# Loading the last two modulation pieces by halves, splitting the first query/key unit by column halves, and one unit load moved ahead of six small loads

## What is computed

```python
ada = jax.nn.silu(c) @ w_ada[l] + b_ada[l]               # 6 x 1024 columns per layer
sh1, sc1, g1, sh2, sc2, g2 = jnp.split(ada, 6, axis=-1)
h = x * (1.0 + sc1) + sh1                                # 256 tokens x 1024
qa, ka, va, qb, kb, vb = jnp.split(h @ w_in, AB_SPLITS)  # queries, keys, values
# attention, output projection, layer norm, feed forward; a second layer; the second block
```

## Time and profile before

| | |
|---|---|
| median of 3 runs | 1247.75 us (1244.14 to 1251.18) |
| the profiled execution | 1245.37 us, its span 1243.7 us |
| TensorE busy | 1200.2 us, 96% of the span |
| VectorE busy | 675.1 us, 54% |
| ScalarE busy | 503.0 us, 40% |
| DMA | 394.98 MB, mean 318 GB/s |
| chain that ended last | PE 84%, DVE 8%, ACT 3%, DMA 3% |

### The profile page before, as it was taken

How to read it: one execution, slowest core, us unless ns; L and a number is a source line. 1 busy time by engine, 2 the same in 40 slices (tenths; PEclk the granted TensorE clock), 3 DMA queues, 4 the chain that set the end, 5 groups by cost and what they waited for, 6 DMA issues and landing times.

```text
span 1243.7 us, 16572 instructions
## 1 busy us (share of the span) xinstructions
PE 1200.2 (96%) x6586; PEld 827.0 (66%) x6586; DVE 675.1 (54%) x1222; ACT 503.0 (40%) x763; POOL 53.8 (4%) x103
## 2 busy tenths in 40 slices
PE   6999899999999999999999999999999999999997
PEld 2697688887789877888878787445544444454446
DVE  5689968887679786764566675211211111111126
ACT  1478654444555575344347384111111111111125
POOL 0100101000000000001001200000000000000000
PEclk9999999999999999999999999999999999999998
DMA  9997868988646455765557779999999999999990
GB/s 368 388 338 275 311 222 307 346 311 324 246 171 249 173 219 184 280 219 204 198 201 269 250 304 397 410 426 426 424 425 425 427 411 425 427 424 426 425 412 35
DMA packets 50987, 394.98 MB, mean 318 GB/s; under 512 B 6673, under 2 KB 8913, under 8 KB 11378
## 3 DMA queue, kind: packets, MB, share of 16 engines
q1 hardware_dynamic: 39618, 337.18, 67.7%
q0 software_dynamic: 9072, 53.92, 12.1%
q10 hardware_dynamic: 2240, 3.10, 1.0%
HBM read 390.68 MB, written 3.49 MB: 317 GB/s over the span
## 4 chain that ended last, share of the span: by engine, by line
PE 84%; DVE 8%; ACT 3%; DMA 3%; issue 1%; SPq 1%; ACTq 0%; DVEq 0%
PE psum L1357 18%; PE psum L770 10%; PE psum L773 10%; PE psum L777 10%; PE psum L1403 9%; PE psum L1289 5%; PE psum L1297 2%; PE psum L825 2%; PE psum L829 2%; PE psum L827 2%; DMA staged<-in_ada 2%; DVE w_parts L2113 2%; DVE aring L2096 1%; PE psum L1056 1%; PE psum L1068 1%; PE psum L1047 1%
## 5 line engine op out<-in xcount | busy, mean ns | idle before, releaser
L2113 DVE TENSOR_TENSOR w_parts<-w_raw,w_parts 128x2048 fp32r<-128x2048 f32 x106 | 241.7, 2287 | 73.1 <-ACT w_parts L1493 73.1
L1493 ACT ACTIVATE w_parts<-w_raw 128x2048 fp32r<-128x2048 f32 x106 | 202.0, 1911 | 80.5 <-DMA w_raw<-in_units 80.5
L1357 PE MATMUL psum<-slabs,arena 128*64 128x512 f32 x768 | 222.5, 592 | 0.0
L770 PE MATMUL psum<-w_parts,h_parts 128*128 128x512 f32 x416 | 165.7, 398 | 2.4 <-ACT h_parts L1493 1.3
L773 PE MATMUL psum<-w_parts,h_parts 128*128 128x512 f32 x416 | 163.2, 392 | 0.0
L1357 PEld LDWEIGHTS psum<-slabs,arena 128*64 128x64 f32 x768 | 71.8, 137 | 109.2 <-issue 109.1
L1493 ACT ACTIVATE arena<-psum 128x512 f32<-128x512 f32 (+1 forms) x43 | 23.8, 557 | 245.4 <-PE psum L1376 140.0
L777 PE MATMUL psum<-w_parts,h_parts 128*128 128x512 f32 x416 | 111.8, 391 | 0.7 <-DVE h_parts L2290 0.7
L2096 DVE CUSTOM_DVE_ANT_0 aring<-aring,cb 128x1024 f32<-128x1024 f32 x80 | 94.5, 1219 | 2.0 <-DMA aring<-in_ada 1.9
L770 PEld LDWEIGHTS psum<-w_parts,h_parts 128*128 128x128 f32 x416 | 78.6, 189 | 20.3 <-DVE w_parts L2113 2.1
L777 PEld LDWEIGHTS psum<-w_parts,h_parts 128*128 128x128 f32 x416 | 78.1, 188 | 17.8 <-DVE h_parts L2290 1.3
(11 more groups left out here) (333 smaller groups left out, 1878.0 us busy)
## 6 DMA issues: line engine op xcount, KB each, us to landing
w_raw<-in_units SPq DMA_DIRECT2D x110, 1024.0 KB, 5.2
slabs<-in_w SPq DMA_DIRECT2D x52, 1024.0 KB, 14.4
slabs<-in_w SPq DMA_DIRECT2D x22, 2048.0 KB, 20.0
aring<-in_ada POOLq DMA_DIRECT2D x40, 1024.0 KB, 5.6
arena<-in_w SPq DMA_DIRECT2D x16, 2048.0 KB, 18.8
w_odd<-in_w SPq DMA_DIRECT2D x16, 2048.0 KB, 19.2
w_odd<-in_w SPq DMA_DIRECT2D x24, 1024.0 KB, 24.1
staged<-in_ada SPq DMA_DIRECT2D x8, 1024.0 KB, 18.6
```

The costliest lines, as they stand in the source:

```text
L770: mm(psum[:, bank, :], high(tile, tok), w_hi(k)[:, col:col + 512], start=first and bank not in begun, stop=False, skip_group_check=True)
L1357: ins = nc.tensor.matmul(psum[s * CAP:(s + 1) * CAP, w, :], xe_t[:, kt, s * CAP:(s + 1) * CAP], up_weights(w, s, b, kt), start=kt == 0, st ...
L1493: return nc.scalar.activation(out_ap, in_ap, func, **kw)
L2113: v.tensor_tensor(w_lo(k), raw(k), w_hi(k).bitcast(F32), ALU.subtract).then_inc(w_split, 1)
```

## The change

Four edits in the opening, with what they need elsewhere.

1. The loads of pieces 6 and 7 are each cut into two transfers of 512 KB (`stage_half(n, t)`, the columns of `t` = 0 and of `t` = 1). The order on SP becomes: half 0 of piece 6, half 0 of piece 7, half 1 of piece 6, unit 3, half 1 of piece 7, unit 4. DVE handles them by halves (`last_scale(0)`, `last_scale(1)`) and gives `scale_ready` 4 for feature tile 6 and 5 for feature tile 7; ACT waits for each tile by itself.
2. `first_values` runs over the two feature tiles outside and the two token tiles inside, so that it needs the second feature tile only for its second half. The event `v_half` comes after three quarters of the last call, where it came after one half.
3. The split of unit 4 is done in two halves by column (128 x 1024 each) on ACT and on DVE; the first half of `to_heads(0, 0, 0)` waits for the first half alone.
4. Unit 5 (with its wait for `unit_done` 1) is issued ahead of the six small loads.

```diff
-            for i in range(4):
+            def stage_half(n, t):
+                col = slice(t * D, (t + 1) * D)
+                sp.dma_start(staged[n][:, col], a["ada"][ADA_ORDER[n]][:, col]).then_inc(last_half_in[n - 6] if t else staged_in[n], 16)
+
+            for i in range(3):
                 stage(2 * i)
...
+            stage_half(6, 0)
+            stage_half(7, 0)
+            stage_half(6, 1)
+            load_unit(3)
+            stage_half(7, 1)
             load_unit(4)
+            load_unit(5)
             small_loads(((lam_in[:], a["lam_in"]), (bias[:, 16, :], a["causal"]), (w_forget[:], a["w_forget"]),
...
-            for k in range(SLOTS, Z_AT):
+            for k in range(SLOTS + 1, Z_AT):
...
-                for t in range(TT):
-                    for s in range(2):
-                        pe.wait_ge(h_first, 2 * i + s + 1)
+                for s in range(2):
+                    pe.wait_ge(h_first, 2 * i + s + 1)
+                    for t in range(TT):
...
+                if k == QK_AT and s:
+                    weights(k)
                 if s == 0:
-                    weights(k)
+                    if k == QK_AT:
+                        pe.wait_ge(first_high, first_high_at)
+                        pe.wait_ge(first_low_half, first_low_at)
+                    else:
+                        weights(k)
...
-                act.wait_ge(scale_ready, p + 1)
                 for kt in (2 * p, 2 * p + 1):
-
+                    act.wait_ge(scale_ready, p + 1 if kt < KT - 1 else p + 2)
...
-            split(4)
+            act.wait_ge(w_loaded[slot_of(4)], 16)
+            for half_s in range(2):
+                ins = A(by_half(w_hi(4), half_s), by_half(raw(4), half_s), Cp)
+                if half_s == 0:
+                    ins.then_inc(first_high, 1)
+            ins.then_inc(w_hi_ready, 1)
...
+            def last_scale(t):
+                for n in (6, 7):
+                    dve.wait_ge(last_half_in[n - 6] if t else staged_in[n], 16)
+                    w = staged[n][:, t * D:(t + 1) * D]
+                    at_ = 2 * (n % 2) + t
+                    v.tensor_tensor_reduce(out=w, in0=w, in1=cb[:], scale=1.0, scalar=0.0, op0=ALU.mult, op1=ALU.add,
+                                           accum_out=ada_raw[:, at_:at_ + 1]).then_inc(ada_sum, 1)
+                dve.wait_ge(ada_sum, 12 + 2 * t + 2)
+                for n in (6, 7):
+                    at_, col = 2 * (n % 2) + t, 2 * ADA_ORDER[n] + t
+                    ins = v.tensor_tensor(ada_cols[:, col:col + 1], ada_raw[:, at_:at_ + 1], V("b_ada", col, 1), ALU.add)
+                    if t:
+                        ins.then_inc(ada_done, 1)
+                    else:
+                        link(ins)
+                if t:
+                    dve.wait_ge(ada_done, 8)
+                v.tensor_scalar(small[:, 6 + t:7 + t], ada[:, 0, 14 + t:15 + t], 1.0, None, ALU.add).then_inc(scale_ready, 1)
+
             first_scale(0)
             for p in range(3):
-                first_scale(p + 1)
+                if p < 2:
+                    first_scale(p + 1)
+                else:
+                    last_scale(0)
                 first_low(p)
...
+            last_scale(1)
             first_low(3)
-            split(4)
+            dve.wait_ge(first_high, first_high_at)
+            v.tensor_tensor(by_half(w_lo(4), 0), by_half(raw(4), 0), by_half(w_hi(4), 0).bitcast(F32),
+                            ALU.subtract).then_inc(first_low_half, 1)
+            dve.wait_ge(w_hi_ready, split_no(4))
+            v.tensor_tensor(by_half(w_lo(4), 1), by_half(raw(4), 1), by_half(w_hi(4), 1).bitcast(F32),
+                            ALU.subtract).then_inc(w_split, 1)
             split(5)
```

More of the change, by code:

```diff
@@ L337, in raw, with by_half @@
             return w_raw[:, slot_of(k), 0, :]
+        def by_half(unit, s):
+            return unit.rearrange("p (k s n) -> p s k n", s=2, n=P)[:, s, :, :]
         def w_lo(k):
@@ L361, in build @@
         scale_ready, h_first = sem("scale_ready"), sem("h_first")
+        first_high, first_high_at = h_first, KT + 1
+        first_low_half, first_low_at = scale_ready, 6
         h_high, h_low = sem("h_high"), sem("h_low")
@@ L424, in build @@
         sg_done, out_ready, stored = sem("sg_done"), [sem("out_ready0"), sem("out_ready1")], sem("stored")
+        last_half_in = (ple_in, late_rows)
         COPIES, BANDS = 32, 16 * P // 32
@@ L806, in first_values @@
                                      skip_group_check=True)
-                    if i == 3 and t == 0:
-                        ins.then_inc(v_half, 1)
+                        if i == 3 and s == 1 and t == 0:
+                            ins.then_inc(v_half, 1)
                 ins.then_inc(unit_done, 1)
@@ L1227, in _ @@
                 from_act(layer, 10, 1)
-            pe.wait_ge(ple_in, 16)
+            pe.wait_ge(ple_in, 32)
             pe.wait_ge(early_rows, 32)
@@ L2927, in _ @@
             root("gate", 1)
-            dve.wait_ge(late_rows, 32)
+            dve.wait_ge(late_rows, 48)
             gated_sum(0, 0, cols[0])
```

## The result

The change made the kernel slower: 1249.65 us, median of 21 runs (1247.06 to 1252.54), against 1244.69 us for the kernel before (1243.37 to 1251.18, 21 runs beside them). The ratio over all runs of both is 1.0035, 95% interval 1.0027 to 1.0043, so 3.4 to 5.4 us are lost where I had forecast a gain of 1.2. The profiled execution has a span of 1246.4 us.

What follows compares the result with a forecast made beforehand. TensorE, busy for 96% of the span, was taken as the bound; of at most 1.87 us direct gain, a lead of 1.5 fell to 1.2: 1245.37 - 1.2 = 1244.2 us profiled, 1246.5 for the median; range 1242.3 to 1250.5.

Steps and rivals of the forecast that it cites:

- my rivals: Whole kernel: lead lost again, 1247.5 us, chance 0.24; more gained, 1245.5, 0.13; transfers cost more, 1250.8, 0.08.
- The halves of pieces 6 and 7: Opening loads: first halves by 34.49, last half 40.3, fourth value call at 39.2 instead of 41.05; lead 1.5 us.
- the slower rival: Opening loads: two more transfers cost 3.6 us, last half lands at 43.9; 2.0 to 3.6 lost, 1250.8 us; chance 0.08.
- Bytes and queue are the same, only the order differs.: Loads of pieces 6 and 7: half a piece takes 1.50 us, against 3.00 for a piece.
- that page's sum per transfer: Skill page: a DMA costs about 2.0 us plus bytes over 436 GB/s; would put unit 4 at 47.0; forecast took zero.
- Then unit 4 at 42.99 as before: Opening loads: after the last half at 40.3, unit 4 lands at 42.99, unchanged.
- that cover: ACT's unit 4 split and first value copy end at 46.0 against PE's need at 46.4; any overrun paid one for one.
- Unit 6 follows the same bytes as before and lands at 53.72: Loads after unit 5 and the small loads: unit 6 split by 57.95 against a need at 58.0, just met.
- The sum: Whole kernel: 1245.37 - 1.2 = 1244.2 us for the profiled execution, 1246.5 for the median; forecast's chance 0.55.
- Column halves, order of the matmuls, extra instructions: Unit 4 split halves 1.0 us on ACT, 1.2 on DVE; same 16 matmuls; extra DVE work (3 x 0.17) mostly in waits.
- I let the 1.2 us stand to the end.: After the first scores: the 1.2 us PE lead becomes a DVE lead near 92 us and lasts to the end.
- What I named as proof against me: Opening: last half after 41, unit 3 holding PE at 39.2, unit 5 near 49, no PE lead at layer norm, 153.

## Why the prediction was wrong

The measured time lies inside the range that I gave, but on the other side of no change, and the mechanism that decided it was none of my rivals. That the range holds it is luck: it reached so far for a fixed cost of each transfer, which did not occur, and for the spread of a median.

- **The halves of pieces 6 and 7.** Right within 0.3 us: both first halves by 34.72 and the last half at 40.41, for 34.5 and 40.3; the fourth call at 39.00 for 39.2, held by unit 3 by 0.19; a call longer by 0.4 (7.49 against 7.10) for a pause of 0.35 in its middle. The last half came before 41.9, so the slower rival, a fixed cost for each transfer, did not occur.
- **"Bytes and queue are the same, only the order differs."** This is the first step that failed. The packets are not the same. On SP's queue 7.1 KB went in a packet with whole pieces, 3.6 KB with halves, and in the same stretch ACT's copy sent a packet for each. I counted bytes on SP's queue and never looked at what ACT's and POOL's queues were waiting for. The Trainium skill has the rule, in DMA: Bandwidth & Descriptors, section Queues, rings and completion order: each DMA engine goes round the queues that have work and takes a packet from each in turn. By that rule the traces agree to one packet in 200. I weighed that page's sum per transfer and passed over this. In that page of the Trainium skill the sum stands in section Anatomy of one DMA, not in Measured as I wrote, and it is for transfers issued from GpSimd, which these were not. The last half at 40.41, for 40.3 from bytes alone, shows no such cost.
- **"Then unit 4 at 42.99 as before".** It was 45.11, by the early bands, whose turns and lower total rate I had no term for; with the bands at 41.32 it was in by 43.54. The lead ended there: ACT's split and its value copy behind it came 1.26 us late for PE. I had put that cover at 0.4 us and named the price, one for one; it was paid. Unit 5 followed 4.6 us after unit 4 where I had 4.3, so its 49.70 for 47.3 is unit 4's delay.
- **"Unit 6 follows the same bytes as before and lands at 53.72"**, and the sentence that the small loads are late "by one unit". Unit 6 came 4.3 us late, and in the traced execution this is the largest wait. In the kernel before the small loads passed at 40 to 44 us, when POOL's transfers had been issued and had not begun; that was their cover, and I named none. Behind unit 5 they ran beside POOL's ring pieces and moved 0.18 MB in 4 us. It is not this part's fault alone: with part 4 undone the ratio was 1.0042, so the halves by themselves lead into the meeting.
- **The sum.** PE's wait for unit 6 was 2.29 us, and the pause cost more than itself: the granted clock of 62 to 67 us, which was 1.00 before, was 0.66, a mean of stretches at 2.4 and at 1.2 GHz:

```profile
62.00:67.00 5.00, 4.70 (x26) 4.57 (x28) 4.86 (x10) 4.00 (x3) 0.54 (x1) 0.66 0.90 341
```

  From 62.30 to the scores at 66.85 are 4.55 us for a half that takes 2.9: 1.65 more. I had no term for this. With the waits of 0.28 and 2.29, and a start on unit 4 that was 0.15 late, it makes up the 4.38.
- **Column halves, order of the matmuls, extra instructions.** Right: two ACT parts in 2.00, DVE 1.23 and 1.22, and parts 2 and 3 alone at 0.9994.
- **"I let the 1.2 us stand to the end."** Right in both directions up to the layer norm: 4.38 us of delay at 62 us was 4.41 at 157, and a lead of 1.26 was 1.25 at 152. To the end it is not shown for a step so small, since later falls of the clock move the distance by some 1.6 us each. With the bands held back and the small loads moved, the changed kernel gained 0.0017, 2.1 us (1.0 to 3.2), for a forecast of 1.2.
- **What I named as proof against me.** Three of the four signs came: unit 3 held PE at 39.0, unit 5 landed near 49 (49.70), and PE came to the layer norm without a lead. The last half did not land after 41.

## What to carry to other kernels

When a transfer is cut or moved, count packets and not only bytes, and look at every queue that is served in the same stretch: whatever becomes ready earlier there will start its own transfers earlier. Small loads are cheap only while nothing else is queued; beside large packets of another queue they hold up all that stands behind them in their own. And one traced execution shows the mechanism, not the usual size of an effect: here the two traces differ by 4.4 us in the opening and by 2.7 in their spans. An order of transfers that happened by itself, here POOL behind ACT's slow copy, should be made a wait before something else is tuned around it; one such wait was worth 0.5% and 0.6% in the two pairs of runs here.

## What the runs showed of the hardware

Two busy queues sent equal numbers of packets, whatever their size: 318 and 318 in 4 us, with 1.16 and 0.49 MB; 191 and 192, with 1.43 and 0.18 MB. Against that, where no other queue had work the 434 KB of small loads hardly slowed their own: with POOL held until they were in, SP's queue sent 807 packets with 2.05 MB in 42 to 47 us, 410 GB/s.

POOL's transfers did not begin when they were issued: the bands were issued at 40.41, and the queue's first packets came in 44 to 45 us; in the changed kernel it was 35.62 and 39 to 40. While the bands ran, the total rate was 256 to 334 GB/s in the kernel before and 281 to 301 in the changed one, against 390 to 420 around them.

The clock of TensorE fell after some short pauses and not after others. The granted clock was 0.66 in 49 to 54 us of the run with the small loads on ACT's queue, behind a pause of 1.90, and 1.00 in 46 to 52 us of the changed kernel, behind one of 1.26:

```profile
49.00:54.00 5.00, 3.96 (x21) 3.99 (x22) 2.52 (x3) 3.99 (x6) 0.00 (x0) 0.66 1.02 417
```

```profile
46.00:52.00 6.00, 4.74 (x38) 4.29 (x36) 2.71 (x3) 4.38 (x7) 0.00 (x0) 1.00 1.03 410
```

In the kernel before, 40 to 46 us, after a pause of 1.87, it was 1.00 as well. With only the halves, a pause of 2.19 us before the fourth call was followed by 0.66 in 41 to 46 us; with the halves and the bands at 40 us, one of 2.21 at the same place by 1.00 in 40 to 46. So pauses of 1.9 to 2.2 us fall on either side, and the length of the pause alone does not decide. What a fall costs was worked out once above: 1.65 us beside the pause of 2.29.
